# One decoder step on one Trainium2 core: borders of stages cut finer, and low parts of attention's weights on GpSimd

## The chip, the cores and the metric

The kernel runs on one core of a Trainium2 chip. The core has TensorE (matmul), VectorE, ScalarE, GpSimd and SyncE, each with its own queue of instructions that it works off in order; they wait for each other through semaphores. The metric is the device time of one execution in microseconds, the median of three runs.

## The reference

Two decoder layers over a prompt of 1024 tokens and 8 samples of 4 tokens, with the same weights, D = 1024:

```python
# every sub-layer: h = h + post_norm(f(pre_norm(h))), RMS norms over D
# layer 0: gated linear attention (4 heads), then ConvFFN
# shared K/V = rms_norm(h, g_kv) @ w_kv
# layer 1: sliding-window (128) softmax attention with sinks, 16 query heads over 2 K/V heads, then ConvFFN
def conv_ffn(x, prev, w_up, conv_w, conv_b, w_down):
    up = x @ w_up
    u, val = up[..., :D_FF], up[..., D_FF:]              # D_FF = 2816
    c = conv_b + sum of conv_w[j] * u shifted by j        # 3 taps along the sequence
    return (gelu(c) * val) @ w_down, last two rows of u
def sink_attend(q, k, v, bias, valid, sinks):
    s = where(valid, q @ k * HD ** -0.5 + bias, -inf)
    m = maximum(max(s), sink)
    p = exp(s - m)
    return (p / (sum(p) + exp(sink - m))) @ v
```

It returns the two outputs, the GLA states, the last conv rows and the K/V windows.

## The kernel before

Everything is held transposed: channels on the 128 partitions, tokens along the row. The 1056 tokens are two halves, X = 0 with 512 columns and X = 1 with 544 (two chunks of 272); a whole activation of a half is 8 planes. A product in fp32 is made of three matmuls in a rounded type (fp32r): each factor is a high part (`w_hi`, `act_hi`) and a low part (the value less its high part), and the product is low*high + high*low + high*high.

**Weights.** They are cut in 366 blocks of 128x1024, in the order that `weight_order` writes out. Each is loaded by SyncE (`w_load`, two raw slots), rounded by ScalarE (`w_round`, L409), and VectorE subtracts (`w_rest`, L414); `w_hi` and `w_lo` have three slots. `round_after(act, name)` and `rest_after(dve, name)` treat the block three places after the named one. `w_load` of a block waits for the `w_lo` of the block two places before it.

**Order of stages on every engine.** A first norm of half 0; eight GLA turns (4 heads for half 0, 4 for half 1); FFN halves f = 0 and 1 (22 tiles each: an up block `u`, a value block `val`; every two tiles a group of down projections with two `d` blocks, `down_unit` L451, added into `acc` by VectorE, `down_add` L463); attention in 64 steps of one head pair and one block of 128 queries, with query projections, output projections (`ao`) and the samples' part between them; FFN halves f = 2 and 3; and a last norm of half 1. `project` (L431) makes all projections that are no down projections.

**Borders.** Between two stages of a half, `acc` is normed, scaled and added to the residual h, which is read back from DRAM, and then normed again to give the next stage's `act_hi` and `act_lo`. This pass of a half runs while the other half is in a stage, in nine numbered steps that hand-written tables (`ACT_GLA`, `DVE_GLA`, `ACT_STEPS`, `DVE_STEPS`, `PE_STEPS`, `ACT_AT`, `DVE_AT`, `PE_AT`) put at turns, tiles and attention steps: 0 and 1 are squares of half of the planes (`act_square`, folded by `dve_fold`), 2 is the sum over partitions by a matmul with ones (`pe_sum`, L509), the root (`act_rstd`) and the load of half of h, 3 the other half, 4 to 6 the same for the next norm, 7 and 8 the normed planes (`dve_norm` L561), their high part (`act_hi` L570) and the low part on GpSimd (`pool_lo`, L574), which has no other work. `dve_post` scales a pair of planes and adds h to it at once:

```python
dve.wait_ge(po_done, 4 * p - 3 + 2 * m + y)
dve.wait_ge(h_in, 32 * (2 * p - 1 + m))
last = nc.vector.tensor_tensor(a, a, NM[X][:, 2 * y:2 * y + 2], ALU.add)
```

At the start SyncE loads constants, x of half 0, two weight blocks, x of half 1, and then writes the bias rows of attention to DRAM, each 128 times (3 MB), before it goes on with weights. Softmax attention is, for one step on VectorE: scores plus bias (L1719), maximum (L1724), its negative (L1726), reciprocal (L1730), and for half of the steps a copy of the sinks (L1713); ScalarE has the exponentials (L1860) and the scaling (L1869).

Of the kernel before, what the change touches and what calls it, by code (L numbers as in the profile page):

```python
# [15 lines left out]
P = 128  # L16
D = 1024
# [53 lines left out]
KH = KT // 2  # L71


def weight_order():
# [12 lines left out]

    put(("glr", 0), W_GLR)
# [4 lines left out]
    for u in range(2 * H):  # L93
# [4 lines left out]
        if u < 2 * H - 1:  # L98
            for what in "qk":
                put((what, u + 1), gla_row(what, (u + 1) % H))  # L100
            for t in range(2):
                put(("v", u + 1, t), gla_row("v", (u + 1) % H, t))
        for t in range(2):
            put(("o", u, t), gla_row("o", u % H, t))

    def ffn(f):
        w0 = (W_F0, W_F1)[f // 2]

        def tile(g, t):
            b = w0 if g == 0 else w0 + 4 + 6 * (g - 1)  # L110
            bt = b + 2 * t + (2 * t if g else 0)
            put(("u", f, 2 * g + t), bt)
            if f == 1 and 2 * g + t == 11:
                for x in range(2):
                    put(("kv", 0, x), W_KV + x)
            put(("val", f, 2 * g + t), bt + 1)

        def downs(g):
            b = w0 + 4 + 6 * g + 2 if g < FG - 1 else w0 + 4 + 6 * (FG - 1)
            for t in range(2):  # L120
                put(("d", f, g, t), b + t)

        tile(0, 0)
        tile(0, 1)
        for g in range(1, FG):
            tile(g, 0)
            downs(g - 1)
            tile(g, 1)
        downs(FG - 1)

    def att():
        def query(q):
            X, p = divmod(q, 8)
            put(("aq", X, p), W_M1 + HW * (p // 4) + p % 4)

        def downs(k):
            X, d = divmod(k, 4)
            for t in range(2):
                put(("ao", X, d, t), W_M1 + HW * (d // 2) + 4 + 2 * (d % 2) + t)

        query(0)
        for k in range(8):
            query(2 * k + 1)
            if k == 2:
                put(("kv", 1, 0), W_KV)
            if k < 7:
                query(2 * k + 2)
            if k == 2:
                put(("kv", 1, 1), W_KV + 1)
            if k:  # L150
                downs(k - 1)
        downs(7)

    ffn(0)
    ffn(1)
    att()
    ffn(2)
    ffn(3)
# [8 lines left out]
def build(nc, wall, xT, gains, ffnpar, wgate, state, kcT, vc, ck, cv, onehot, masks, smask, bmask,  # L167
# [10 lines left out]
    with ctx:  # L178
# [30 lines left out]
        EPSC = place("eps_col", [P, 1])  # L209
# [2086 lines left out]
```

## Time and profile before

| | |
|---|---|
| median of three runs | 2797.86 us (2793.33 to 2800.45) |
| profiled execution | 2794.6 us, its span 2792.8 us |
| TensorE busy | 2521.1 us, 90% |
| VectorE busy | 1654.8 us, 59% |
| ScalarE busy | 1140.4 us, 41% |
| GpSimd busy | 85.5 us, 3% |
| mean granted TensorE clock | 0.955 |
| DMA | 255 MB, 91 GB/s |

The span goes from the first to the last instruction; a row of a timeline gives start, duration, engine (a q behind it marks its sequencer, where DMAs are issued), line, operation, tiles and count, and in brackets how long the engine had been idle before it and who ended that. "issue" means that the profile shows nothing that ended the wait.

### The profile page before, as it was taken

What the parts mean: (1) busy time and instruction counts of PE and PEld (TensorE: products, weight loads), DVE (VectorE), ACT (ScalarE), POOL (GpSimd) and SP (SyncE); (2) the same over time, 40 slices, a digit from 0 to 9 for tenths busy, and PEclk for the clock granted to TensorE, in tenths of its full rate; (3) what the DMA queues carried; (4) which work ended last, traced back from release to release, by engine and by line L of the source; (5) the groups of instructions that cost most, each with busy time, mean ns of one, the idle gap of its engine ahead of it and who ended that gap; (6) DMA issues with size and microseconds to landing.
All of it is one profiled execution on the core that took longest, in us unless ns stands there. A gap on an engine that the chain in (4) does not pass through costs nothing.

```text
span 2792.8 us, 37637 instructions
## 1 busy us (share of the span) xinstructions
PE 2521.1 (90%) x15437; PEld 2206.9 (79%) x15437; DVE 1654.8 (59%) x2811; ACT 1140.4 (41%) x1792; POOL 85.5 (3%) x22
## 2 busy tenths in 40 slices
PE   2999999998999999999997889878999999999994
PEld 1777888887778879999995666667777888999994
DVE  2677556665665555765555666665665555655554
ACT  2555444343443324333334656553443333333232
POOL 0000000000010000010000110000001000000000
PEclk8999999988999999999998899989999999999997
DMA  7222213322422323323223222221332232332222
GB/s 153 78 67 76 84 63 101 106 85 81 155 78 96 98 76 96 133 74 99 84 84 100 74 90 76 67 93 34 107 129 91 93 98 79 106 118 80 88 91 75
DMA packets 93799, 255.17 MB, mean 91 GB/s; under 512 B 10947, under 2 KB 44204, under 8 KB 91820
## 3 DMA queue, kind: packets, MB, share of 16 engines
q1 hardware_dynamic: 69916, 209.24, 24.1%
q10 hardware_dynamic: 23712, 43.52, 4.4%
q8 instruction: 123, 2.02, 0.3%
q14 instruction: 48, 0.39, 0.0%
HBM read 225.92 MB, written 26.74 MB: 90 GB/s over the span
## 4 chain that ended last, share of the span: by engine, by line
PE 39%; DVE 5%; ACT 4%; issue 3%; DMA 1%; POOL 1%; ACTq 0%; DVEq 0%
PE banks L431 23%; PE banks L451 13%; DMA normed<-h_scratch 1%; ACT w_hi L409 1%; DVE w_lo L414 1%; PE banks L1569 1%; PE banks L1543 1%; ACT probs L1860 1%; PE banks L1555 1%; POOL act_lo L574 1%; DVE normed L561 0%; ACT act_hi L570 0%; DVE hf L1371 0%; DVE stats L1724 0%; ACT normed L488 0%
## 5 line engine op out<-in xcount | busy, mean ns | idle before, releaser
L431 PE MATMUL banks<-act_hi,w_lo 128*128 128x272 f32 (+1 forms) x2952 | 977.1, 331 | 49.5 <-DVE act_lo L574 21.1
L431 PE MATMUL banks<-act_hi,w_hi 128*128 128x272 f32 (+1 forms) x2952 | 963.1, 326 | 0.0
L431 PE MATMUL banks<-act_lo,w_hi 128*128 128x272 f32 (+1 forms) x2952 | 961.8, 326 | 0.0
L409 ACT ACTIVATE w_hi<-w_raw 128x1024 fp32r<-128x1024 f32 x366 | 380.5, 1055 | 778.8 <-PE banks L451 518.4
L414 DVE TENSOR_TENSOR w_lo<-w_raw,w_hi 128x1024 fp32r<-128x1024 f32 x366 | 464.8, 1283 | 375.9 <-ACT w_hi L409 375.7
L431 PEld LDWEIGHTS banks<-act_hi,w_lo 128*128 128x128 f32 x2952 | 562.5, 191 | 112.9 <-issue 27.4
L431 PEld LDWEIGHTS banks<-act_lo,w_hi 128*128 128x128 f32 x2952 | 563.5, 191 | 44.0 <-issue 1.7
L431 PEld LDWEIGHTS banks<-act_hi,w_hi 128*128 128x128 f32 x2952 | 561.7, 190 | 44.0
L463 DVE TENSOR_TENSOR acc<-acc,banks 128x272 f32<-128x272 f32 (+1 forms) x624 | 315.9, 518 | 216.5 <-PE banks L451 212.5
L451 PE MATMUL banks<-h_hi,w_lo 128*128 128x272 f32 (+1 forms) x1056 | 354.9, 336 | 59.0 <-issue 36.1
L451 PE MATMUL banks<-h_lo,w_hi 128*128 128x272 f32 (+1 forms) x1056 | 351.4, 333 | 0.0
L451 PE MATMUL banks<-h_hi,w_hi 128*128 128x272 f32 (+1 forms) x1056 | 351.3, 333 | 0.0
L451 PEld LDWEIGHTS banks<-h_hi,w_lo 128*128 128x128 f32 x1056 | 205.9, 195 | 84.5 <-issue 39.3
L451 PEld LDWEIGHTS banks<-h_lo,w_hi 128*128 128x128 f32 x1056 | 207.4, 196 | 17.0
L451 PEld LDWEIGHTS banks<-h_hi,w_hi 128*128 128x128 f32 x1056 | 205.7, 195 | 16.4
L574 POOL TENSOR_TENSOR act_lo<-normed,act_hi 128x2176 fp32r<-128x2176 f32 (+1 forms) x18 | 85.3, 4739 | 2042.5 <-ACT act_hi L570 2042.5
L1425 ACT ACTIVATE u<-banks 128x512 f32<-128x512 f32 (+2 forms) x132 | 59.0, 451 | 170.7 <-PE banks L431 167.0
L1438 ACT ACTIVATE c<-u,par 128x512 f32<-128x512 f32 (+1 forms) x88 | 73.1, 830 | 95.0 <-issue 89.5
L1860 ACT ACTIVATE probs<-scores,stats 128x257 f32<-128x257 f32 (+1 forms) x128 | 62.4, 489 | 76.9 <-PE banks L1555 39.2
L1348 DVE SCALAR_TENSOR_TENSOR c<-u,par,c 128x512 f32<-128x512 f32 (+1 forms) x88 | 68.0, 773 | 43.1 <-ACT c L1438 43.1
L451 PE MATMUL banks<-o_hi,w_lo 128*128 128x272 f32 (+1 forms) x192 | 68.7, 358 | 23.7 <-DVE acc L463 9.1
L1869 ACT ACTIVATE probs<-probs,stats 128x256 f32<-128x256 f32 (+1 forms) x128 | 56.3, 489 | 68.1 <-DVE stats L1730 67.4
(209 smaller groups left out, 2657.8 us busy)
## 6 DMA issues: line engine op xcount, KB each, us to landing
w_raw<-wall SPq DMA_DIRECT2D x366, 512.0 KB, 3.6
normed<-h_scratch ACTq DMA_DIRECT2D x12, 704.0 KB, 4.7
h_scratch<-acc ACTq DMA_DIRECT2D x3, 2176.0 KB, 8.5
h_scratch<-acc ACTq DMA_DIRECT2D x3, 2048.0 KB, 8.3
gstates<-state ACTq DMA_DIRECT2D x4, 1024.0 KB, 6.2
gla_s<-gstates ACTq DMA_DIRECT2D x4, 1024.0 KB, 4.0
bias<-bias_scratch SPq DMA_DIRECT2D x32, 128.0 KB, 3.6
bias_scratch<-bias_rows SPq DMA_DIRECT2D x1, 3064.0 KB, 36.6
```

Source lines behind the costliest of these rows:

```text
L409: nc.scalar.activation(WH[:, b % RING], WR[:, b % RAW], ACT.Copy).then_inc(w_hi, 1)
L414: nc.vector.tensor_tensor(WL[:, b % RING], WR[:, b % RAW], WH[:, b % RING].bitcast(fp32), ALU.subtract).then_inc(w_lo, 1)
L431: last = nc.tensor.matmul(PS[:, bank, 0:n], w, a[X][:, k, o:o + n], start=(k == 0 and first), stop=(k == KT - 1 and w is wh and a is AH))
L451: last = nc.tensor.matmul(PS[:, bank, 0:w_], w, a[t][:, o:o + w_], start=(t == 0 and x == 0), stop=(t == 1 and x == 2))
L463: nc.vector.tensor_tensor(a, a, PS[:, bank, 0:w_], ALU.add).then_inc(dn_add, 1)
L574: engine.tensor_tensor(AL[X][:, part(m)], NM[X][:], AH[X][:, part(m)].bitcast(fp32), ALU.subtract).then_inc(al_done, 1)
L1348: nc.vector.scalar_tensor_tensor(C[:, 0:cv], U[:, 1:1 + cv], PAR[:, t, 17:18], C[:, 0:cv], ALU.mult, ALU.add).then_inc(cv1, 1)
L1425: last = nc.scalar.activation(U[:, 2 + o:2 + end], PS[:, bank, 0:end - o], ACT.Copy)
L1438: nc.scalar.activation(C[:, 0:cv], U[:, 2:2 + cv], ACT.Identity, bias=PAR[:, t, 19:20], scale=PAR[:, t, 18:19]).then_inc(cb, 1)
L1543: last = nc.tensor.matmul(PS[:, e, x0:2 * WIN], Q1[x, q % 2, i * WIN:(i + 1) * WIN], KG[x, q % 8 // 4, (blk - 1) * WIN + x0:(blk + 1) * WI ...
L1860: last = nc.scalar.activation(EX[:, u, e, x0:], SS[:, u, e, x0:], ACT.Exp, bias=ST[:, r, 2 + e:3 + e], accum_out=ST[:, r, 4 + e:5 + e])
L1869: last = nc.scalar.activation(x, x, ACT.Copy, scale=ST[:, g % 8, 6 + e:7 + e])
```

## The change

- **Start.** The first norm has functions of its own (`act_first_norm`, `dve_first_norm`, `pe_first_norm`): x comes in quarters, each fold goes to a matmul of its own, and the normed planes are made in quarters. The load of half 1's x stands behind the loads of blocks `("v", 0, 0)` and `("r", 0, 0)`; the bias rows have a place of their own in SBUF and are written two at a time from tile 2 of f = 0 on.
- **Joins.** The first `u` and `val` blocks of f = 0 and f = 2 stand before the last down projections of the stage ahead (`pe_first_block`). The last down group of f = 0 and f = 2 stands after the first tile of the next half; that of f = 1 after attention's first query.
- **Passes.** Scaling and residual are separate steps (`dve_scale`, `dve_residual`), h is loaded in quarters, the steps have names, and the tables place them anew; K and V of half 0 move from tile 11 to 13.
- **Attention.** From the second query block on to the last step, GpSimd subtracts the low parts of the weights (`pool_att`, 31 blocks) and its own `pool_lo` of that stage stands in the same queue.
- **End.** The last down group goes chunk by chunk, with squares, sums, root, results and stores by chunk; h of the last pass is loaded ahead into `act_lo`.

```diff
-        def act_h_load(act, i, X, m):
-
-            if m:
-                act.wait_ge(ha_done, 2 * POSTS[i, X] - 1)
+        def act_h_load(act, i, X, y):
+
+            p = POSTS[i, X]
+            if y < 2:
+                act.wait_ge(ps_done, 2 * NORMS[i, "post", X])
             else:
...
+                act.wait_ge(ha_done, 4 * p - 5 + y)
...
+        def dve_residual(dve, i, X, y):
+            p = POSTS[i, X]
+            dve.wait_ge(po_done, 4 * p - 3 + y)
+            dve.wait_ge(h_in[y % 2], 32 * (2 * p - 1 + y // 2))
+            a = ACC[X][:, pair(y)]
+            nc.vector.tensor_tensor(a, a, NM[X][:, pair(y % 2)], ALU.add).then_inc(ha_done, 1)
...
+                else:
+                    pe.wait_ge(os_ev, h + 1)
+                    pe_first_block(pe, 0, "u", FIRST)
...
+                else:
+                    pe_first_block(pe, 0, "u", SECOND)
+                    pe.wait_ge(gq_ms, u + 1)
+                    pe_first_block(pe, 0, "val", ALL)
...
-        PE_STEPS, DVE_STEPS = {3: 2, 7: 6}, {1: 0, 2: 1, 4: 2, 5: 3, 6: 4, 7: 5, 8: 6, 9: 7}
-        ACT_STEPS = {0: 0, 1: 1, 3: 2, 4: 3, 5: 4, 6: 5, 7: 6, 8: 7, 9: 8}
+        PE_FFN = {3: "sum", 9: "Sum"}
+        DVE_FFN = ({1: ("f0",), 2: ("f1",), 4: ("s0", "s1"), 5: ("a1", "s2", "s3"), 6: ("a3",), 7: ("F0",), 8: ("F1",),
+                    10: ("n0a", "n0b"), 11: ("n1a", "n1b")},
+                   {4: ("a0",), 5: ("a2",)})
+        ACT_FFN = ({1: ("sq1",), 3: ("root",), 5: ("h3",), 6: ("Sq0",), 7: ("Sq1",), 9: ("Root",), 10: ("hi0",), 11: ("hi1",)},
+                   {0: ("sq0",), 2: ("h0", "h1"), 4: ("h2",)})
...
+            pool.wait_ge(w_lo, BLK["aq", 0, 1] + RING)
+            for s in range(NIT + 1):
+                k, w = divmod(s, 8)
+                if w == 2:
+                    rest_after(pool, ("aq", (2 * k + 1) // 8, (2 * k + 1) % 8), nc.gpsimd)
+                    if k == 2:
+                        rest_after(pool, ("kv", 1, 0), nc.gpsimd)
+                elif w == 4 and k < 7:
+                    rest_after(pool, ("aq", (2 * k + 2) // 8, (2 * k + 2) % 8), nc.gpsimd)
+                    if k == 2:
+                        rest_after(pool, ("kv", 1, 1), nc.gpsimd)
+                elif w == 0 and k >= 2:
+                    for t in range(2):
+                        rest_after(pool, ("ao", (k - 2) // 4, (k - 2) % 4, t), nc.gpsimd)
+                if s in POOL_LO:
+                    pool_lo(pool, *POOL_LO[s])
...
-            sp.wait_ge(rb_row, 1)
-            sp.dma_start(r_dram.rearrange("(h p m) -> h p m", p=P, m=RL),
-                         RB[:].unsqueeze(1).broadcast_to([NQ, P, RL])).then_inc(rb_out, 16)
...
+        def dve_first_norm(dve):
+            for y in range(4):
+                dve.wait_ge(e_sq, y + 1)
+                x = NM[0][:, pair(y % 2)]
+                if y >= 1:
+                    dve.wait_ge(e_ss, y)
+                nc.vector.tensor_tensor(RS[0][:], x[:, 0], x[:, 1], ALU.add).then_inc(e_f, 1)
...
+            pe.wait_ge(w_lo, BLK["d", 3, FG - 1, 1] + 1)
+            pe.wait_ge(hl, FT * 4)
+            for m in range(2 * KT):
+                if m == KT + KH:
+                    sums(0)
+                down_unit(pe, 1, LAST_DOWNS, m, [BLK["d", 3, FG - 1, t] for t in range(2)],
+                          [HH[:, t] for t in range(2)], [HL[:, t] for t in range(2)], 4 + m % 4, 4)
+            sums(1)
```

## Rows read from the trace of the kernel before

**Rows 1.** The page's section 1: busy time by engine, share of the span, instructions.
```profile
PE 2521.1 (90%) x15437; PEld 2206.9 (79%) x15437; DVE 1654.8 (59%) x2811; ACT 1140.4 (41%) x1792; POOL 85.5 (3%) x22
```

**Rows 2.** Busy time in stretches: start:end, length, busy us (instructions) by engine, granted clock, DMA.
```profile
0.00:62.00 62.00, 13.05 (x28) 7.87 (x29) 19.20 (x23) 15.75 (x12) 0.20 (x4) 0.81 0.79 168
...
653.00:1489.00 836.00, 799.14 (x4816) 718.85 (x4814) 494.62 (x798) 299.16 (x393) 28.18 (x6) 0.98 0.30 96
...
1489.00:1915.00 426.00, 346.87 (x2278) 264.57 (x2278) 268.21 (x542) 248.62 (x596) 28.47 (x6) 0.92 0.25 79
...
1915.00:1946.00 31.00, 24.73 (x195) 21.96 (x196) 14.47 (x35) 9.33 (x22) 0.00 (x0) 0.89 0.11 35
...
2756.00:2793.00 37.00, 2.18 (x4) 1.17 (x4) 15.67 (x18) 7.97 (x6) 0.00 (x0) 0.54 0.37 120
```

**Rows 3.** TensorE's waits over the span: us in total, times, longest.
```profile
PE banks L451 <- issue: 50.3, 15, 8.1
...
PE banks L1569 <- DVE o_lo L1737: 24.6, 6, 6.7
```

**Rows 4.** DMA issues up to us 70, and the timeline of the start.
```profile
bias_scratch<-bias_rows SPq DMA_DIRECT2D x1, 3064.0 KB, 36.6
...
18.41 2.05 PE L509 MATMUL banks<-rstd,ones 128*128 128x512 f32 x2 [12.75 <-DVE rstd L503]
...
23.15 2.74 DVE L561 SCALAR_TENSOR_TENSOR normed<-acc,gain_cols,rstd 128x512 f32<-128x512 f32 x4 [4.89 <-ACT rstd L517]
...
57.06 0.80 PE L431 MATMUL banks<-act_hi,w_lo 128*128 128x512 f32 x1 [21.10 <-DVE act_lo L574]
...
62.24 0.39 PE L431 MATMUL banks<-act_hi,w_lo 128*128 128x512 f32 x1
```

**Rows 5.** TensorE's timeline at the GLA join, and the chain around us 2150.
```profile
639.07 0.57 PE L451 MATMUL banks<-go_hi,w_lo 128*128 128x272 f32 x1 [8.12 <-issue]
...
2142.37 22.30 PE banks L431 x96
```

**Rows 6.** Timelines of TensorE and VectorE in the FFN halves.
```profile
720.45 1.29 DVE L549 TENSOR_TENSOR acc<-acc,normed 128x1088 f32<-128x1088 f32 x1 [1.73 <-DMA normed<-xT]
...
725.70 0.77 PE L451 MATMUL banks<-h_hi,w_lo 128*128 128x512 f32 x1 [4.94 <-issue]
...
780.63 0.70 PE L509 MATMUL banks<-rstd,ones 128*128 128x272 f32 x2 [1.89 <-DVE rstd L503]
...
831.49 4.55 DVE L414 TENSOR_TENSOR w_lo<-w_raw,w_hi 128x1024 fp32r<-128x1024 f32 x1 [2.65 <-ACT w_hi L409]
...
2416.71 0.36 PE L451 MATMUL banks<-h_hi,w_lo 128*128 128x272 f32 x1 [4.29 <-issue]
```

**Rows 7.** Attention from us 1489 to 1946: shares of the chain, then two rows of timelines.
```profile
by line: PE banks L431 18.2%; PE banks L451 16.6%; issue 7.1%; DMA normed<-h_scratch 4.6%; PE banks L1569 4.3%; PE banks L1543 3.6%; ACT probs L1860 3.6%; PE banks L1555 3.3%; DVE stats L1724 2.5%; DVE w_lo L414 2.2%; DVE scores L1719 2.2%;
...
1539.84 0.69 PE L1569 MATMUL banks<-probs_t,v_tok 128*64 128x128 f32 x4 [6.68 <-DVE o_lo L1737]
...
1807.61 1.22 DVE L549 TENSOR_TENSOR acc<-acc,normed 128x1024 f32<-128x1024 f32 x1 [6.74 <-DMA normed<-h_scratch]
```

**Rows 8.** Groups by shape (GpSimd, VectorE), then the timeline beside two GpSimd instructions.
```profile
L574 POOL TENSOR_TENSOR act_lo<-normed,act_hi 128x2048 fp32r<-128x2048 f32 x8 | 36.6, 4578 | 1084.7 <-ACT act_hi L570 1084.7
...
L414 DVE TENSOR_TENSOR w_lo<-w_raw,w_hi 128x1024 fp32r<-128x1024 f32 x366 | 464.8, 1283 | 375.9 <-ACT w_hi L409 375.7
...
1633.43 4.80 POOL L574 TENSOR_TENSOR act_lo<-normed,act_hi 128x2176 fp32r<-128x2176 f32 x1 [33.96 <-ACT act_hi L570]
...
1634.07 4.19 DVE L1713 COPY scores<-sinks_b 128x2 f32<-128x2 f32 x1
...
1651.24 2.82 DVE L1726 TENSOR_SCALAR stats<-stats 128x2 f32<-128x2 f32 x1
```

**Rows 9.** Timeline of the tail.
```profile
2756.17 2.02 ACT L488 ACTIVATE normed<-acc 128x2176 f32<-128x2176 f32 x1 [15.05 <-DVE acc L463]
...
2778.44 10.40 ACTq L1484 DMA_DIRECT2D yT<-acc  x4
```

More of the change, by code:

```diff
@@ L71 @@
 KH = KT // 2
+KV_TILE = 13
 def weight_order():
@@ L102, in weight_order @@
                 put(("v", u + 1, t), gla_row("v", (u + 1) % H, t))
+        if u == 2 * H - 1:
+            ffn_tile(0, 0)
         for t in range(2):
             put(("o", u, t), gla_row("o", u % H, t))
[L106 to L158, printed above, removed]
+    def ffn_layer(l):
+        for f in (2 * l, 2 * l + 1):
+            for t in range(FT):
+                if f % 2 or t:
+                    ffn_tile(f, t)
+                if t % 2 == 0 and t:
+                    ffn_downs(f, t // 2 - 1)
+                elif t == 0 and f % 2:
+                    ffn_downs(f - 1, FG - 1)
+    def query(q):
+        X, p = divmod(q, 8)
+        put(("aq", X, p), W_M1 + HW * (p // 4) + p % 4)
+    def att_downs(k):
+        X, d = divmod(k, 4)
+        for t in range(2):
+            put(("ao", X, d, t), W_M1 + HW * (d // 2) + 4 + 2 * (d % 2) + t)
@@ L159, in weight_order @@
+    ffn_layer(0)
+    query(0)
+    ffn_downs(1, FG - 1)
+    for k in range(8):
+        query(2 * k + 1)
+        if k == 2:
+            put(("kv", 1, 0), W_KV)
+        if k < 7:
+            query(2 * k + 2)
+        if k == 2:
+            put(("kv", 1, 1), W_KV + 1)
+        if k:
+            att_downs(k - 1)
+    ffn_tile(2, 0)
+    att_downs(7)
+    ffn_layer(1)
+    ffn_downs(3, FG - 1)
     return names, rows
@@ L1209, in turn @@
                     nc.scalar.activation(O[:, :, HP:WM], PS[:, 0:2, 0:SAMP], ACT.Copy).then_inc(os_ev, 1)
+                for step in gla_steps(ACT_GLA, u, "outputs"):
+                    act_step(act, *step, 0)
                 if more:
@@ new lines, in dve_ffn, with act_ffn_downs_done @@
+                if f % 2 or t:
+                    rest_after(dve, ("val", f, t))
+                product(f, t)
+                group = ffn_group(f, t)
+                if group is not None:
+                    dve_ffn_adds(dve, *group)
+                    for x in range(2):
+                        rest_after(dve, ("d", *group, x))
+                dve_ffn_lo(dve, f, t)
+        def act_ffn_downs_done(act, f, g):
+            act.wait_ge(dn_full, dn_end((f, g)))
+            for t in range(2):
+                round_after(act, ("d", f, g, t))
```

779 lines of the change are left out of this document (464 added, 315 removed), and 6 rows, old and new, of tables (DVE_AT, DVE_GLA).

## The prediction

> **What bounds the kernel now.** The page's first section comes first: TensorE is busy 2521.1 of 2792.8 us [rows 1]. No matmul is removed (the last sum of squares is cut finer), so what can be won is the 272 us in which TensorE is idle, less what the change costs. The table by stretch shows where these are [rows 2]: 49 of the first 62 us, 37 in the first FFN layer (653 to 1489), 79 in attention (to 1915), 6 where it drains, and 35 of the last 37; the other 66 lie in the GLA turns and the second FFN layer. VectorE is busy 63% and ScalarE 58% of attention: neither is full, so attention waits on chains between engines. The list of what TensorE waited for says what ends the waits [rows 3]: 15 waits of 50.3 us in sum stand in front of down projections, where the profile names no releaser, and 24.6 us in attention are for o_lo. The longest were then followed in the timeline.
>
> **Start.** The 3 MB write of the bias rows takes 36.6 us and is issued at 14.03 us. The weight loads are behind it on SyncE's queue, so the third block is late. ScalarE rounds it ahead of the second half of act_hi, and TensorE stands 21.10 us until 57.06; the first query projection starts at 62.24 [rows 4]. The change writes the rows in eight parts inside the first FFN and lifts the second half's inputs behind two weight loads. I retrace the start with the same rows. x comes in four quarters; folds (0.7 us for two planes of 512) and sums (2.05 us a matmul) alternate, because each fold waits for the sum before it: four rounds of about 2.9 us from us 7.5 on end at 19, against 20.5 now. Root with one table load brings rstd at 21.6. VectorE then has eight norm steps (2.74 us per four), four low parts and one weight low part of 1024 columns (1.28 us each) and a memset: 12.4 us, so query(0) starts near 34. Gain 28, less 1 to 2 for a TensorE that is not warm: 27 (22 to 30).
>
> **Joins of stages.** The last GLA down projection waits 8.12 us for normed outputs [rows 5]. Now the first FFN up and value blocks stand ahead of it, 48 matmuls; 96 take 22.30 us [rows 5], so 11.1 us of work. Half of `u` stands before the sum of squares and delays the chain by 2.8 us, and the low part of the second half of act_hi ends some 0.7 us after it is wanted. The downs then start at 642.8, not 639.1: 11.1 - 3.7 = 7.4, plus 1 because the matmuls behind the wait start slow (0.57 us for 272 columns): 8.5 (6 to 10). Inside each FFN layer the last down group (4.43 and 4.44 us) now has the next half's first tile in front: 8 (6 to 9). Into attention (4.65) a query projection of 5.6 us covers it: 4.5 (3 to 6). Out of attention the window of 31 us holds 6.3 idle [rows 2] and 11.1 us of work to put there: 6 (3 to 7). The last of these waits (3.14) stays.
>
> **Tile 4 of each FFN half.** The four waits there are 4.94, 4.11, 4.97 and 4.29 us, first and last in [rows 6]. VectorE meets the residual's load (1.73 us of wait at 720.45), and four more steps and the weight's low part stand behind it before TensorE resumes at 725.70. The change starts the load at tile 2, puts the root ahead in tile 3, and lets only the scaling stand before the weight's low part: 16 of 18.3 (12 to 18). The second sum of squares moves from tile 7 to 9: 4.5 of the 5 us of rows like the one at 780.63 (3 to 5). At tile 10 and in the second half's norm steps a weight low part is held by GpSimd (4.55 us at 831.49, with 3.17 us of TensorE wait behind it, twice; smaller ones in the second half, 9 in sum) [rows 6]. The new order puts the weight ahead of act_hi, but conv now meets GpSimd: 6 (-2 to 10).
>
> **Attention, loads.** The chain of the 457 us from 1489 on has 4.6% on the residual's load, 21 us; VectorE waits 6.74 us for it at 1807.61, and TensorE 6.68 us at 1539.84, the last of three waits of 16.3 us there [rows 7]. Loads now start two and six steps ahead of the root and stand in quarters: 19 (10 to 22).
>
> **Attention, GpSimd.** 31 weight low parts leave VectorE. All 366 have a mean of 1283 ns, so 40 us; on the chain they hold 2.2%, 10 us [rows 7]. GpSimd takes 4578 ns for 2048 columns [rows 8], so 2.3 us for 1024, 71 us in all. No row shows GpSimd on weights, but its five long instructions of attention show the price beside VectorE. While one runs (1633.43 to 1638.23), a two-element copy that has a median of 148 ns takes 4.19 us and ends with it; the sign change of the maxima takes 2.82 us at 1651.24 instead of 0.17 [rows 8]. Additions from PSUM that start beside it keep their length. So a short VectorE instruction, which every softmax step has on its chain, stands for the rest of a GpSimd instruction. I laid 2.3 us behind each of the 31 roundings in the trace, the first at 1504.98 and the last at 1919.30: 14 meet such an instruction, and the delays sum to 21.4 us. As half of VectorE's work there is on the chain, 11 lost against 10 won: 0 (-21 if all count and nothing is won, to +10). A weight block itself is not late: three slots lie ahead of TensorE, and a projection takes 5.6 us.
> The Trainium skill, "SBUF — State Buffer", section "Who interferes with whom", calls the ports of the two engines one exclusive lock, held for a whole instruction, and lets a VectorE instruction with one SBUF input and no two-port mode pass; the trace agrees (4.19 us in the place of 0.15). It speaks against this part of the change: that is the first rival below.
>
> **Tail.** From the last matmul of the downs, 37 us pass [rows 2]: two squares of 2.02 and folds (9.6 us in all until the sum), a load that waits for the buffer, four scale-and-add pairs with a second load, then a 1.1 MB store [rows 9]. Now the downs run chunk by chunk. The first chunk's squares, sum and root lie under the second's (1.8 us of sum matmuls stand between them), the residual is loaded 14 us early, and behind the last matmul are one add, one square, eight results, one fold and a store of a quarter. A result is two steps of 272 columns and an add of 544, from neighbours 0.48 and 0.72 us: 1.8 with latency. 1.2 + 8 x 1.8 + 0.5 + 2.5 = 18.6, plus 1.8: 20.4. Gain 16 (13 to 19).
>
> **Small costs.** ScalarE issues 25 more DMAs (0.48 us each, 12 us over all stages, mostly where it idles over 40%). Eight parts of the bias write take 4.6 us each, a weight load 3.6, and a load has two blocks of 5.6 us: covered. If not, each costs up to 1. I take -2 (0 to -8).
>
> **Sum.** 27 + 8.5 + 8 + 4.5 + 6 + 16 + 4.5 + 6 + 19 + 0 + 16 - 2 = 113.5. The profiled execution took 2794.6 (1.8 around its span), so 2681; the median is 3.3 above it: 2684. All low ends give 47, all high ends 146: 2652 to 2751.
>
> **Rivals.**
> *The lock decides attention.* Every instruction that meets GpSimd waits on the chain, and the work taken off VectorE wins nothing: 21.4 us, 2705. Where two low parts follow each other behind the output blocks, 4.6 us at once, up to 10 more. For it: the two waits in [rows 8]. Against: in 17 of 31 places nothing meets it. 2705 to 2715, chance 0.17.
> *Waits are only displaced.* Finer steps make more waits between in-order engines; half of tile 4, the sums and the loads (45 us) comes back: 23. For: the profile shows which wait ended last, not the next one. 2707, chance 0.13.
> *VectorE was the pace of attention.* 24.6 us of TensorE's waits there are for o_lo [rows 3], and the shared queue delays the additions too; with 40 us less work ahead of them another 27, two thirds of it, go. 2657, chance 0.13.
> *Slower than before.* GpSimd's low part is wanted by the third next block and frees the raw slot; if VectorE's two-input instructions keep it from starting and each weight is late by more than 113.5 / 31 = 3.7 us, the gain is gone; at 5 us it is 2839. Against: its 18 instructions now last 4.5 to 4.9 us with VectorE beside them. Chance 0.03.
>
> **Numbers.** The forecast has 0.54: 2684, by itself 2668 to 2700. The range reaches to the lock and to the quick attention: 2652 to 2732. A measurement tells about 0.3%, 8 us, from no change. Every case but the last is over 60 us faster: faster 0.96, same 0.01, slower 0.03.
>
> **What would show it.** Query projections from us 34; no TensorE wait over 2 us at tile 4 and at the joins; no wait for h_scratch in attention; about 20 us behind the last down matmul. GpSimd would show 31 instructions of 2.3 us, and VectorE's two-element instructions a tail up to 2.3 us; attention (query to the last output block) near 415 us. If these stand and attention is above 430, the lock decided; if the FFN layers keep over 50 us of idle TensorE together, the waits moved.

## The result, and the profile after

The changed kernel takes 2753.86 us (median of 4 runs, 2746.97 to 2759.79) against 2798.76 (2793.33 to 2800.45) for the kernel before, now of four runs: ratio 0.9842, 95% interval 0.9815 to 0.9869. It is 45 us faster, where 114 were forecast; the range (2652 to 2732) missed it by 22 us. The profiled execution took 2752.62 with a span of 2750.7.

Section 1 of the page after, beside [rows 1]:

```profile
PE 2532.1 (92%) x15455; PEld 2214.3 (81%) x15455; DVE 1660.6 (60%) x2796; ACT 1147.1 (42%) x1810; POOL 160.7 (6%) x53
```

TensorE is idle 219 us, 53 less than before, but it is busy 11 us longer, with hardly any work added. The table by stretch, cut at the last addition of each stage: start, the four feed-forward networks (the FFN halves f = 0 to 3) with attention between the second and third, tail. The GLA turns, 40.1 to 626.6, are left out here.

```profile
0.00:40.10 40.10, 23.09 (x59) 12.11 (x60) 18.88 (x25) 18.65 (x21) 0.20 (x4) 1.00 0.49 161
626.60:1023.80 397.20, 380.65 (x1645) 308.02 (x1644) 234.06 (x304) 146.92 (x178) 10.10 (x2) 0.98 0.35 109
1023.80:1447.90 424.10, 410.72 (x3147) 404.12 (x3145) 266.28 (x493) 151.23 (x215) 18.34 (x4) 0.99 0.29 94
1447.90:1949.50 501.60, 392.19 (x2498) 305.12 (x2499) 281.81 (x544) 259.82 (x619) 103.11 (x37) 0.87 0.23 70
1949.50:2328.40 378.90, 374.34 (x1646) 304.31 (x1645) 233.98 (x304) 147.30 (x178) 10.11 (x2) 1.00 0.34 106
2328.40:2733.90 405.50, 395.36 (x3079) 392.11 (x3079) 236.87 (x473) 136.81 (x208) 0.00 (x0) 0.99 0.30 96
2733.90:2750.70 16.80, 1.88 (x6) 0.59 (x4) 13.19 (x26) 4.83 (x8) 0.00 (x0) 0.67 0.41 133
```

The same cuts of the kernel before, and what each stage won once the work that moved over a border is allowed for. The moved work is priced with [rows 5]: 96 matmuls in 22.30 us, so 11.15 for a first tile of 48 and 5.57 for a query projection of 24. A first tile of a second half (96 short matmuls) is 12.06. "Combined" is the best of the first experiments; it comes below.

| stage | before | after | won | forecast | combined | won |
|---|---|---|---|---|---|---|
| to the first query copy | 68.0 | 40.1 | 27.9 | 27 | 40.3 | 27.7 |
| GLA | 585.3 | 586.5 | 10.0 | 8.5 | 585.5 | 11.0 |
| network 1 | 394.0 | 397.3 | -2.4 | | 380.1 | 14.8 |
| network 2 | 441.8 | 424.0 | 11.3 | | 423.9 | 11.4 |
| attention | 457.1 | 501.6 | -38.9 | 25 | 463.5 | -0.8 |
| network 3 | 393.0 | 378.9 | 15.0 | | 379.8 | 14.1 |
| network 4 | 416.9 | 405.5 | -0.7 | | 405.3 | -0.5 |
| four networks together | | | 23.2 | 39 | | 39.8 |
| tail | 36.7 | 16.8 | 19.9 | 16 | 16.8 | 19.9 |

(39 are the terms 8, 16, 4.5, 6 and the 4.5 of the join into attention, whose wait stood ahead of network 2's last additions. 25 are the loads' 19 and the 6 out of attention.) The columns sum to 42 and, with the small costs of -2, to 113.5. So start, GLA and tail came near their terms, and networks 2 to 4 together won 25.6. Two places lost: **network 1**, and **attention**.

*Network 1.* SyncE, ScalarE and TensorE in the timeline behind the first bias part:

```profile
626.97 0.76 SPq L1273 DMA_DIRECT2D bias_scratch<-bias_rows  x1
628.48 32.23 SPq L410 DMA_DIRECT2D w_raw<-wall  x6
660.75 0.65 SPq L1273 DMA_DIRECT2D bias_scratch<-bias_rows  x1
...
645.99 1.06 ACT L415 ACTIVATE w_hi<-w_raw 128x1024 fp32r<-128x1024 f32 x1 [4.69 <-DMA w_raw<-wall]
...
681.15 1.06 ACT L415 ACTIVATE w_hi<-w_raw 128x1024 fp32r<-128x1024 f32 x1 [5.67 <-DMA w_raw<-wall]
...
648.35 0.79 PE L437 MATMUL banks<-act_hi,w_lo 128*128 128x512 f32 x1 [5.53 <-DVE w_lo L420]
...
695.94 0.77 PE L460 MATMUL banks<-h_hi,w_lo 128*128 128x512 f32 x1 [3.45 <-issue]
```

The weight issued at 628.48, right behind the part, is there at 645.99: 17.5 us for a load that takes some 4. TensorE stands 5.5 us until 648.35, and 3.5 until 695.94.

*Attention.* What TensorE waited for there (us in total, times, longest):

```profile
PE banks L460 <- DVE acc L472: 21.2, 8, 5.7
PE banks L437 <- ACT rstd L520: 14.2, 2, 7.1
PE banks L1719 <- DVE s_scores L1867: 12.9, 2, 6.8
PE banks L437 <- issue: 10.3, 2, 9.6
PE banks L1617 <- issue: 8.8, 1, 8.8
...
PE banks L1643 <- DVE o_lo L1821: 4.9, 3, 1.8
```

The wait for o_lo, 24.6 us in [rows 3], is down to 4.9, as forecast. The first five rows have taken its place. The 8.8 us stand ahead of the first scores, and the 9.6 us ahead of the keys and values of step 16. GpSimd's group for the weights, beside [rows 8]:

```profile
L420 POOL TENSOR_TENSOR w_lo<-w_raw,w_hi 128x1024 fp32r<-128x1024 f32 x31 | 74.8, 2426 | 417.3 <-ACT w_hi L415 417.3
```

31 instructions of 2.4 us, as forecast (2.3). Two of them stand beside VectorE's chain of the sample softmax:

```profile
1766.77 4.64 POOL L420 TENSOR_TENSOR w_lo<-w_raw,w_hi 128x1024 fp32r<-128x1024 f32 x2 [26.04 <-ACT w_hi L415]
...
1767.28 1.86 DVE L1856 TENSOR_TENSOR s_stats<-s_stats,s_sinks 128x1 f32<-128x1 f32 x1
1769.17 2.26 DVE L1858 TENSOR_TENSOR s_stats<-s_sinks,s_stats 128x1 f32<-128x1 f32 x1
...
1775.04 0.57 PE L437 MATMUL banks<-act_hi,w_lo 128*128 128x272 f32 x1 [7.15 <-ACT rstd L520]
```

One-column instructions, 0.16 us each in the kernel with VectorE's low parts (e1, below), end with GpSimd's two instructions. Behind them ScalarE makes the exponentials and then the root, and TensorE waits 7.15 us for the root, where the same wait in the kernel before was 3.3.

### The profile page after: what moved, and what is told of

It reads as the page before. It is cut to its first block and busy times, and to the rows that moved or that the text cites. A ratio compares the mean times of both kernels' runs of the same rounds, so it can differ in the third digit from the quotient of the medians.

```text
span 2750.7 us, 37795 instructions
## 1 busy us (share of the span) xinstructions
PE 2532.1 (92%) x15455; PEld 2214.3 (81%) x15455; DVE 1660.6 (60%) x2796; ACT 1147.1 (42%) x1810; POOL 160.7 (6%) x53
## 5 line engine op out<-in xcount | busy, mean ns | idle before, releaser
L437 PE MATMUL banks<-act_hi,w_lo 128*128 128x272 f32 (+1 forms) x2952 | 985.8, 334 | 51.1 <-ACT rstd L520 14.2
L420 DVE TENSOR_TENSOR w_lo<-w_raw,w_hi 128x1024 fp32r<-128x1024 f32 x335 | 432.2, 1302 | 391.3 <-ACT w_hi L415 391.0
L437 PEld LDWEIGHTS banks<-act_hi,w_lo 128*128 128x128 f32 x2952 | 568.5, 193 | 116.7 <-issue 59.0
L437 PEld LDWEIGHTS banks<-act_lo,w_hi 128*128 128x128 f32 x2952 | 569.4, 193 | 44.2 <-issue 1.7
L437 PEld LDWEIGHTS banks<-act_hi,w_hi 128*128 128x128 f32 x2952 | 567.6, 192 | 44.6
L460 PEld LDWEIGHTS banks<-h_lo,w_hi 128*128 128x128 f32 x1056 | 204.9, 194 | 16.3
L420 POOL TENSOR_TENSOR w_lo<-w_raw,w_hi 128x1024 fp32r<-128x1024 f32 x31 | 74.8, 2426 | 417.3 <-ACT w_hi L415 417.3
```

The costliest lines, as they stand in the source:

```text
L420: engine.tensor_tensor(WL[:, b % RING], WR[:, b % RAW], WH[:, b % RING].bitcast(fp32), ALU.subtract).then_inc(w_lo, 1)
L437: last = nc.tensor.matmul(PS[:, bank, 0:n], w, a[X][:, k, o:o + n], start=(k == 0 and first), stop=(k == KT - 1 and w is wh and a is AH))
L460: last = nc.tensor.matmul(PS[:, bank, 0:w_], w, a[t][:, o:o + w_], start=(t == 0 and x == 0), stop=(t == 1 and x == 2))
```

## The experiments

All ran beside the kernel before. Ratios are to it.

| run | median us (range) | ratio, 95% interval |
|---|---|---|
| after | 2753.9 (2747.0 to 2759.8) | 0.9842, 0.9815 to 0.9869 |
| e1_dve_low | 2720.6 (2717.8 to 2724.1) | 0.9722, 0.9709 to 0.9735 |
| e2_bias_16rows | 2733.0 (2731.4 to 2738.9) | 0.9770, 0.9756 to 0.9785 |
| e3_before_gpsimd | 2833.4 (2830.3 to 2835.6) | 1.0123, 1.0110 to 1.0137 |
| e4_sp_join | 2745.8 (2742.8 to 2750.6) | 0.9813, 0.9798 to 0.9827 |
| e5_combined | 2696.3 (2694.2 to 2699.9) | 0.9629, 0.9604 to 0.9655 |
| e6_pool_order | 2741.4 (2740.7 to 2745.2) | 0.9792, 0.9766 to 0.9817 |
| e7_lock_alone | 2735.2 (2734.6 to 2740.2) | 0.9771, 0.9745 to 0.9797 |
| e8_bias_start | 2752.7 (2749.7 to 2757.4) | 0.9827, 0.9801 to 0.9852 |
| e9_no_gpsimd | 2690.2 (2687.0 to 2696.1) | 0.9621, 0.9602 to 0.9640 |
| e10_late_loads | 2694.7 (2688.8 to 2697.7) | 0.9630, 0.9611 to 0.9649 |
| e11_loads_step5 | 2700.7 (2699.0 to 2704.6) | 0.9648, 0.9632 to 0.9664 |
| e12_bias_4rows | 2752.9 (2748.6 to 2754.4) | 0.9830, 0.9814 to 0.9847 |
| e13_loads_halves | 2704.6 (2698.2 to 2709.8) | 0.9656, 0.9632 to 0.9680 |
| e14_bias_8rows | 2734.0 (2728.5 to 2735.0) | 0.9758, 0.9738 to 0.9778 |
| e15_gpsimd_ordered | 2714.6 (2711.2 to 2717.3) | 0.9689, 0.9670 to 0.9709 |

### GpSimd in attention

**Low parts back on VectorE** (e1), in the changed kernel:

```
 # pool_att
-                if w == 2:
-                    rest_after(pool, ("aq", ...), nc.gpsimd)
...
 # dve_att, behind biased(s)
+                if w == 2 and k < 8:
+                    rest_after(dve, ("aq", (2 * k + 1) // 8, (2 * k + 1) % 8))
...
```

> The changed kernel with the low parts of the attention's weights subtracted on VectorE again, at the places in its order where the kernel before has them; everything else stays, GpSimd's activation low parts too. Theory (GpSimd's lock on VectorE's small operations and its own order of work cost the attention): the attention, 501.6 us from the end of the second feed-forward network in the changed kernel, falls by 30 to 45 us, the kernel from 2754 to 2710 to 2724; VectorE's work runs long by 30 us instead of 67. Rival (the rewritten tables and the added work of the first tile cost it, not GpSimd): the attention stays within 8 us, kernel 2746 to 2762. Rival of the forecast (GpSimd helps, VectorE is the pace): the kernel gets slower, over 2762.

Measured 2720.6: 33 us less, in attention (501.6 to 470.6 us). The theory holds; the rival that GpSimd helps has the wrong sign. Over the whole kernel VectorE's instructions still run long by 52 us, not 30 (each instruction's length over the median of its shape, where it is over by a quarter and 0.1 us, summed; 67.5 in the changed kernel, 30.2 before). 16 of the 52 lie in attention, where the kernel before had 8: the new order puts more short ones beside GpSimd's six remaining low parts. The other 36 lie outside attention, where the kernel before had 23.

**The kernel before with that alone** (e3): `rest_after` on GpSimd, all borders as before.

> The kernel before with one thing of the change: the low parts of the attention's weights on GpSimd, in the place of its order that the change gives them; all borders stay as before. Theory (lock and in-order queue cost): slower than before by 20 to 40 us, 2818 to 2840, all of it between the end of the second network and the end of the attention. Forecast's own term (no cost, from 21 us of gain to 10 us of loss): 2778 to 2808. If the loss is under 10 us here and over 30 in the run with VectorE's low parts, then GpSimd's cost comes only together with the new order of steps.

Measured 2833.4, 35 us slower, all of it in attention (457.1 to 492.5 us). GpSimd's cost is the same in both orders of steps, 33 and 35 us; the forecast had it at 0.

**The lock by itself** (e7), on top of e1:

```
+            def idle_low(b):
+                pool.wait_ge(w_hi, b + RING + 1)
+                for _ in range(2):
...
+                    nc.gpsimd.tensor_tensor(DM[:], DM[:], DM[:], ALU.subtract)
```

> The changed kernel with the low parts of the attention's weights on VectorE, and GpSimd made to do, at the same places of its order and released by the same high parts, two subtractions of 128x512 each on a spare tile that nobody reads or waits for, where it had one low part of 128x1024. Nothing depends on them, so what they cost over the run with VectorE's low parts alone (2721) is their presence beside VectorE, not their lateness. Theory (most of GpSimd's cost is that VectorE's instructions are held while it works): 8 to 20 us over 2721, 2729 to 2741, and VectorE's instructions run over by 15 to 40 us more than in that run. Rival (its cost is that the low parts come later, in order and 2.4 us long): within 5 us of 2721.

Measured 2735.2: 14.5 us over e1, with VectorE's instructions long by 74.5 us in place of 51.9. GpSimd was busy somewhat longer with the idle work than with the real one (87.0 us in 62 instructions against 74.8), so by this run the lock's share of the 33 is 12 to 15 us. But the idle instructions are 1.1 to 1.4 us long and let VectorE in sooner than the real ones of 2.4. The two statistics of the sample softmax that took 1.86 and 2.26 us in the changed kernel, here:

```profile
1760.34 4.46 POOL L1939 TENSOR_TENSOR idle<-idle 128x512 f32<-128x512 f32 x4 [24.59 <-ACT w_hi L418]
...
1760.84 0.55 DVE L1859 TENSOR_TENSOR s_stats<-s_stats,s_sinks 128x1 f32<-128x1 f32 x1
1761.43 0.16 DVE L1861 TENSOR_TENSOR s_stats<-s_sinks,s_stats 128x1 f32<-128x1 f32 x1
```

TensorE's two waits for the root sum to 6.1 us in place of 14.2. So 12 to 15 is what the lighter work costs, and the real one may cost more; e15 below bears on it.

**One entry of GpSimd's order** (e6):

```
-        POOL_LO = {13: (2, "kv", 1, 0), 15: (2, "kv", 1, 1), ...
+        POOL_LO = {13: (2, "kv", 1, 0), 16: (2, "kv", 1, 1), ...
```

> The changed kernel with one entry of GpSimd's own order moved: the low part of the second half of the attention's key and value activations comes behind the two weight low parts of step 16, not ahead of them. Theory (GpSimd works in its written order, and a weight low part that is ready waits behind an activation low part that isn't): the stall of 9.6 us ahead of the keys and values at step 16 falls to 3 to 6, the kernel from 2754 to 2747 to 2751. Rival (that stall is the lock's, or is paid again two steps later): the stretch from step 16 to step 24 stays at 76 us, and the kernel at 2752 to 2757.

GpSimd's timeline in the changed kernel, and then in e6, with TensorE's wait behind it:

```profile
1547.80 4.77 POOL L581 TENSOR_TENSOR act_lo<-normed,act_hi 128x2176 fp32r<-128x2176 f32 x1 [6.12 <-ACT act_hi L577]
1552.53 4.66 POOL L420 TENSOR_TENSOR w_lo<-w_raw,w_hi 128x1024 fp32r<-128x1024 f32 x2
...
1554.97 0.56 PE L437 MATMUL banks<-act_hi,w_lo 128*128 128x272 f32 x1 [9.62 <-issue]
```

```profile
1542.80 5.67 POOL L420 TENSOR_TENSOR w_lo<-w_raw,w_hi 128x1024 fp32r<-128x1024 f32 x2 [2.67 <-ACT w_hi L415]
1548.42 4.85 POOL L581 TENSOR_TENSOR act_lo<-normed,act_hi 128x2176 fp32r<-128x2176 f32 x1
...
1545.74 0.36 PE L437 MATMUL banks<-act_hi,w_lo 128*128 128x272 f32 x1 [1.94 <-issue]
```

The high parts were rounded by 1545.2. In the changed kernel GpSimd is idle, waiting for act_hi, until 1547.80, and takes the weights only after that low part. One number moved in a table takes the wait from 9.6 to 1.9 us and 12.4 us off the kernel, more than expected. In the profile attention falls from 501.6 to 490.9 us:

```profile
1449.20:1940.10 490.90, 389.31 (x2498) 303.01 (x2499) 289.80 (x545) 259.65 (x619) 104.24 (x37) 0.89 0.23 72
```

Idle time is 7.8 us less, and 7.7 of it is this wait; the same 2498 matmuls take 2.9 us less, at a mean granted clock of 0.89 in place of 0.87.

### The bias parts

**Sixteen rows a part** (e2):

```
-            sp.dma_start(r_dram.rearrange(...)[first:end],
-                         RB[first:end].unsqueeze(1).broadcast_to([end - first, P, RL])).then_inc(rb_out, 16)
+            sp.dma_start(r_dram.rearrange(...)[:, 8 * first:8 * end],
+                         RB[:].unsqueeze(1).broadcast_to([NQ, 8 * (end - first), RL])).then_inc(rb_out, 16)
```

> The changed kernel with the eight parts of the bias cut the other way: each part reads all 16 head rows and writes 16 of the 128 copies, where it read 2 rows and wrote all 128 copies; bytes and places are the same. Theory (a part that reads two partitions only is slow at its source, some 18 us a piece, and the weight loads of the first network wait behind it): a part takes 5 to 9 us, the first network falls from 397 to 383 to 388 us, kernel 2739 to 2745. Rival (the write into DRAM or the sum of bytes is what holds the weights up): parts still take over 14 us and the kernel stays at 2751 to 2757. Rival (the first network loses by its GpSimd low parts and the halo copy at tile 10): the parts get shorter and the first network stays within 4 us.

Measured 2733.0, 21 us less; a part lands in 5.7 us by the page; network 1 falls from 397.3 to 379.9. The theory holds, and the gain is larger than expected: 17.4 of the 21 us are in network 1, where TensorE's waits of 0.9 us and more fall from 15.6 to 5.6 us in sum. That is what is left without any part there (5.4 in e8, below).

**Four rows and eight rows** (e12, e14; `RB[h:h + 4]` to 64 copies, `RB[h:h + 8]` to 32):

> The changed kernel with each of the eight parts of the bias reading 4 of the 16 rows and writing 64 of the 128 copies; bytes and places are the same. Theory (a part takes as long as the rows that it reads from let it: two rows some 17 us, sixteen rows 6): a part holds the weight loads up half as much, the first network falls to 384 to 392 us, kernel 2738 to 2748. Rival (any part with fewer than 16 rows costs the same, or only 2 rows are slow): the first network at 397, or at 380, us.

> The changed kernel with each of the eight parts of the bias reading 8 of the 16 rows and writing 32 of the 128 copies; bytes and places are the same. With 2 and with 4 rows the first network took 397 us, with 16 rows 380. Theory (rows that lie next to each other share one way out at some 25 GB/s, whatever number of transfer engines reads them): 397 again, 2750 to 2756. Rival (it depends on how many rows or engines a part has, with a step between 4 and 16): 380 to 390 us, 2733 to 2745.

Four rows: 2752.9, network 1 at 397.4, as with two. Eight rows: 2734.0, network 1 at 380.0, as with sixteen. My theory for four (time in proportion to rows) fell, and so did the one for eight (neighbours always share). Windows in which nearly nothing but a part is on its way, in the changed kernel (2 rows), with 4 rows and with 8; the last two numbers are the DMA engines' mean share and GB/s:

```profile
640.00:644.00 4.00, 2.82 (x13) 1.95 (x11) 2.62 (x3) 1.30 (x3) 0.00 (x0) 1.00 0.12 26
```

```profile
640.00:644.00 4.00, 4.00 (x19) 3.14 (x17) 2.26 (x3) 2.72 (x3) 0.00 (x0) 1.00 0.21 25
```

```profile
634.00:636.00 2.00, 2.00 (x10) 1.64 (x9) 1.24 (x2) 0.55 (x2) 0.00 (x0) 1.00 0.44 50
```

26 and 25 GB/s for two and four rows, 50 for eight: the rate doubles from four rows to eight and not from two to four. A part is 256 packets of 1532 bytes in the trace; from the first to the last of them pass 13 to 15 us with two rows, 14 with four, 6 to 7 with eight and 3 to 4.5 with sixteen. The Trainium skill, "SBUF — State Buffer", section "Door 1: The DMA port swizzle", has four neighbouring partitions on one of 16 ports of about 27 GB/s each; the trace agrees, with 25 and 26 GB/s for one such group and 50 for two. The Trainium skill, "DMA: Bandwidth & Descriptors", section "Why a DMA increments its semaphore by 16 and not by 1", takes the largest number of transfer engines, at most 16, that divides the outermost dimension of both sides; the shares of 0.12, 0.21 and 0.44 for two, four and eight rows are near 2, 4 and 8 of 16.

**One piece at the start** (e8): the eight parts gone, one write of all rows behind the first loads.

> The changed kernel with the bias written in one piece behind the first loads, where the kernel before has it, in place of eight parts in the first network. Theory (it holds up the first weights at the start, and the eight parts hold them up in the first network): the first query copy of the first layer moves from 40.1 to 46 to 58 us, the first network falls from 397 to 381 us, so the kernel comes to 2740 to 2755. Rival (the start's gain of 28 us comes from the finer steps of the first norm alone): first query copy at 40 to 43 us and the kernel near 2738.

Measured 2752.7, the changed kernel's time. The first query copy comes at 58.8 us, and network 1 is at 379.7. So what moving the write won (18.7 us) its eight narrow parts lost again (17.6). Of the start's 27.9 us 18.7 are the write's; the other 9.2 are those of the finer steps and of the second half's inputs, which e8 leaves behind the two weight loads. Which of the two has how much is not shown.

### SyncE's wait

**One block later** (e4):

```
-                elif name == ("aq", 0, 2):
+                elif name == ("aq", 0, 3):
                     sp.wait_ge(cn, FT * 2)
```

> The changed kernel with one thing moved on SyncE: its wait for the last weight low part users of the second network and the seven loads behind it (bias rows, masks) stand after the load of the next attention query block, not ahead of it. Theory (the first scores wait 8.9 us for the high parts of the last down projection's successor block, whose load is queued behind this wait): the stall ahead of the first score falls from 8.9 us to 2 to 4, kernel shorter by 4 to 7 us, 2747 to 2750. Rival (the masks and bias of the first steps then come later and the first steps wait for them instead): no difference, 2752 to 2756, with a new wait on a DMA in the first three steps.

SyncE's, ScalarE's and TensorE's timeline in the changed kernel, then TensorE's in e4:

```profile
1447.43 1.75 SPq L2086 DMA_DIRECT2D bias<-bias_scratch  x4
...
1450.65 6.63 SPq L410 DMA_DIRECT2D w_raw<-wall  x3
...
1454.61 1.06 ACT L415 ACTIVATE w_hi<-w_raw 128x1024 fp32r<-128x1024 f32 x1 [6.12 <-DMA w_raw<-wall]
1455.57 0.58 ACT L1954 ACTIVATE q<-banks 128x512 f32<-128x512 f32 x1
...
1456.25 0.80 PE L1617 MATMUL banks<-kg,q 64*128 64x128 f32 x4 [8.85 <-issue]
```

```profile
1454.50 0.80 PE L1617 MATMUL banks<-kg,q 64*128 64x128 f32 x4 [2.62 <-issue]
```

In the changed kernel the first query's block stands ahead of the last down blocks in the order of weights. Their rounding makes ScalarE round one block further on, and SyncE issues that one only after its wait for the last down group and seven loads. The query's copy is behind that rounding. Measured 2745.8, 8 us less, of which this wait is 6.2.

### All three, and what is left

**Combined** (e5: e1, e2 and e4).

> The changed kernel with three edits together: the attention's weight low parts back on VectorE, the parts of the bias read from 16 rows each, and SyncE's wait and seven loads one block later. Theory (three separate causes in three stages): their gains of 33.2, 20.9 and 8.1 us add up, 2692, from 2685 to 2699; the attention near 466 us, the first network near 381 us. Rival (the gains overlap, since a stall taken away only moves the wait): above 2702.

2696.3: the gains add, to within 4 us. This is 102 us below the kernel before.

**The change's GpSimd, repaired** (e15: e2, e4, e6).

> The changed kernel as it is, GpSimd with the attention's weight low parts, with three repairs: GpSimd's own order (the key and value low part behind the two weight low parts of step 16), the bias parts of 16 rows and SyncE's wait one block later. Theory (gains add, and GpSimd then costs what the lock takes and the later low parts of the last steps): 2753.9 less 12.4, 20.9 and 8.1 is 2712, from 2706 to 2718, 16 us over the same kernel with VectorE's low parts (2696). Rival (once the queue is in order GpSimd is no worse than VectorE): 2693 to 2700.

2714.6: with its queue in order GpSimd still costs 18 us over VectorE. TensorE's waits in attention, where e5 has 6.5 us for the root and 8.0 for the samples' scores:

```profile
PE banks L437 <- ACT rstd L520: 14.3, 2, 7.2
PE banks L1719 <- DVE s_scores L1867: 12.9, 2, 6.8
```

That is 12.7 us more. The first stands again behind statistics of 1.86 and 2.26 us, and ahead of the second a fold of VectorE's takes 3.40 us beside GpSimd's two instructions and 1.22 without them. The only wait for a low part of GpSimd's is 4.2 us, where VectorE's low part was waited for 3.1. So these traces lay most of the 18 us to held instructions, and some 1 us to low parts that come later.

**No GpSimd in attention** (e9: e5 with `lo_rest(nc.vector, dve, ...)` for the six activation low parts too).

> The combined kernel (attention's weight low parts on VectorE, bias parts of 16 rows, SyncE's wait one block later; 2696) with the six low parts of the activations in the attention on VectorE as well, one step later each; GpSimd does nothing in the attention. Theory (what is left of the attention's excess is partly VectorE's instructions held by GpSimd's six low parts of 4.8 us: the copy of the sinks of 3.9 us at step 60, a statistics instruction of 2.8 us): VectorE takes 15 us of work more and loses some 20 us of delays, the stall of 5.7 us at step 60 falls to 2 or less; 2688 to 2695. Rival (VectorE's added work takes the place of the delays): 2696 to 2704.

2690.2, the lowest median; its interval overlaps e5's, so the runs do not tell the two apart. In the profile attention is 457.1 us against 463.5, as long as in the kernel before, and the wait at step 60 went from 5.7 to 2.0 us.

**Loads behind the root** (e10), **at the old steps** (e11), **in halves at the old steps** (e13), each on e5:

```
-        ACT_AT = {0: ("sq0",), 1: ("sq1",), 2: ("h0", "h1"), 3: ("root",), 5: ("h2",), 6: ("h3",), ...
+        ACT_AT = {0: ("sq0",), 1: ("sq1",), 3: ("root", "h0", "h1"), 5: ("h2",), 6: ("h3",), ...           # e10
+        ACT_AT = {0: ("sq0",), 1: ("sq1",), 3: ("root",), 5: ("h0", "h1"), 6: ("h2", "h3"), ...            # e11
+        ACT_AT = {0: ("sq0",), 1: ("sq1",), 3: ("root",), 5: ("h0", "h1"), 7: ("h2", "h3"), ...            # e13
```

The second pass (steps 38 to 60) is changed alike. e10 issues the first loads two steps ahead of where the kernel before has them. e13 also has VectorE wait for both quarters of a half, and in the first pass puts two of its additions one step later.

> The combined kernel (2696) with the loads of the first two quarters of the stored activations behind the root of the norm in both passes of the attention, as the kernel before has them, in place of ahead of it. Theory (the forecast's term for the loads: they were late for VectorE, and earlier issue removes its waits): VectorE waits for them again and the value products wait behind it, 8 to 19 us over 2696, 2704 to 2715. Rival (the early loads bought nothing, the stalls moved elsewhere anyway): within 4 us of 2696.

> The combined kernel (2696) with the loads of the stored activations issued at the very steps of the kernel before: the first two quarters at steps 5 and 49, the last two at steps 6 and at 50 and 51. (The run with the loads behind the root left them two steps earlier than that, and VectorE never waited.) Theory (the forecast's term for the loads is right in kind): VectorE waits for them again, as the kernel before did for 4.0, 2.3, 6.7 and 1.4 us in the attention, and 5 to 14 us of it reach the end, 2701 to 2710. Rival (TensorE's idle time moves to other waits whether they are there or not): within 4 us of 2696.

> The combined kernel (2696) with the stored activations loaded by halves and as late as in the kernel before: two quarters at a time, at steps 5 and 7 and at 49 and 51, the sums on VectorE waiting for both quarters of a half. Theory (the forecast's term is right in kind and too large, since in the second pass other waits follow that cover it): 5 to 10 us over 2696, 2701 to 2706, nearly all of it in the first pass (steps 0 to 24), and VectorE waits for the loads about 14 us, as before. Rival (the whole term of 19 us is there, and something else in the attention eats it): 12 to 20 us, 2708 to 2716.

VectorE's waits for the load in e11, in e13, and in attention before, where the second row is its wait for GpSimd:

```profile
DVE acc L556 <- DMA normed<-h_scratch: 5.1, 2, 4.3
```

```profile
DVE acc L558 <- DMA normed<-h_scratch: 9.2, 3, 4.3
```

```profile
DVE acc L549 <- DMA normed<-h_scratch: 14.4, 4, 6.7
DVE normed L561 <- POOL act_lo L574: 9.7, 2, 5.6
```

e10 costs nothing: issued two steps before they are wanted the loads are there. e11 costs 4 us. e13 brings 9 us of VectorE's 14 back and costs 8 us by the medians but 1.2 by the profiled spans, and its interval overlaps e5's. In the profiles attention alone is 463.5 us in e5 and e10, 466.9 in e11 and 467.2 in e13, so 3.4 and 3.7 us more. The term is between 1 and 8 us; 19 lies above all three, though none brings all 14 us of VectorE's waits back.

## Why the prediction was wrong

**Start (27), GLA join (8.5), tail (16): right.** 27.9, 10.0 and 19.9 by the table. At the GLA join the wait of 8.12 us is gone; but the GLA stage, which no experiment but e8 touches, is between 581.9 (e9) and 591.7 us (e4) long in the other profiles, so the 10.0 is known to some 5 us. Of the tail's 20.4 us the forecast had 18.6 behind the last down matmul; they were 17.3, because a result takes 1.6 us, not 1.8.

**Networks (39): right in the sum, but for the small costs.** Combined they won 39.8. Only 30 of these are idle time (65.0 us before, 34.6 in the combined kernel, in the four together); the other 9.5 are matmuls that took less time, in networks 1 and 3 at a mean granted clock of 1.00 where it was 0.98. The forecast had added up waits alone, so that its sum fits is in part luck. In the combined kernel the four waits at tile 4, those of the second sum and the two inside the layers are gone, and so is the one of 3.2 us at tile 10 of networks 1 and 3. But the first tiles of these two now wait 4.9 and 4.5 us for a weight's low part, and network 2 keeps two waits for additions, 4.6 and 3.5 us, where it had five smaller ones of 8.9 in sum. The step that failed stands under "small costs": "eight parts of the bias write take 4.6 us each ... covered". That was an eighth of the 36.6 us of [rows 4], and so took the rate of 16 rows for a part of two. A part runs at 25 GB/s, so 13 to 15 us, and the weight behind it comes 14 us late: 21 us lost by the medians, 17.4 in network 1 (e2), where at most 8 were allowed.

**Join into attention: a new wait was not seen.** The forecast had a query projection cover 4.65 us; it did, but did not follow ScalarE's extra rounding to SyncE's queue, where the loads of bias and masks stand ahead of that block. 8 us (e4).

**Attention, GpSimd (0): wrong, and the largest term: -33.** Two errors. The first is the balance of 11 us lost against 10 won. With GpSimd's queue in order and the real low parts the loss is 18 us (e15), near the 21.4 us that the 14 meetings summed to; that only half of it is on the chain was assumed. The 10 us won by taking the work off VectorE show in no run: even with the queue in order attention is 17 us longer than with the weights' low parts on VectorE. Whether the gain was nothing or was eaten, no run separates. The second: "a weight block itself is not late: three slots lie ahead" left out what stands ahead of it in GpSimd's own order. e6 gave 12.4 us back with one entry moved. 18 and 12.4 leave 3 of the 33 us, less than the runs tell apart.

**Attention, loads (19): wrong, 1 to 8.** The views that it rested on were read one step too far. The chain's 21 us are more than all of VectorE's waits for the load, 14.4 us. Of the three waits of 16.3 us up to 1539.84 the first, 4.2, was for ScalarE's probabilities, and it is still there (4.9 us in the combined kernel). Two of the six waits for o_lo (3.5 and 5.9 us) had behind them VectorE's 9.7 us for GpSimd's low part, not the load. And in the second pass VectorE's longest wait, 6.74 us [rows 7], was worth only 2.5 us to TensorE, behind which waits for additions and roots of 3 to 4 us followed whether the load was early or not. The attention of the combined kernel, and the waits in it that replace the one for o_lo:

```profile
1429.80:1893.30 463.50, 384.76 (x2498) 297.77 (x2499) 290.99 (x576) 259.89 (x619) 28.43 (x6) 0.91 0.24 75
```

```profile
PE banks L460 <- DVE acc L472: 20.7, 8, 5.7
PE banks L1719 <- DVE s_scores L1867: 8.0, 2, 4.2
...
PE banks L1643 <- DVE o_lo L1821: 4.5, 3, 1.8
```

The same stretch before:

```profile
1489.10:1946.20 457.10, 371.80 (x2474) 286.71 (x2475) 282.81 (x574) 258.05 (x618) 28.47 (x6) 0.92 0.24 76
```

20 us of waits for o_lo went, and idle time fell from 85.3 to 78.7 us only: waits for additions rose from 14.2 to 23.2 us, those for s_scores from 6.1 to 8.0. The 5.7 us at step 60 are the clearest: before, VectorE waited there for GpSimd to let go of a buffer; now the copy of the sinks is held 3.9 us by the same low part. Against these 6.6 us stands a busy time 7.4 us longer than the 5.6 us of added matmuls, at a mean clock of 0.91 between the two levels, 0.92 before. Why it fell is not settled.

**Out of attention (6): wrong, about 1.** From VectorE's last scores to the end of attention TensorE is idle 7.2 us before and 6.4 in the combined kernel. The first tile's blocks stand behind the wait for s_scores (3.8 us in both) in TensorE's order, so they lengthen the stretch and do not fill it.

**The rivals.** The lock rival named the place and, by e15, nearly the price of the lock alone (21.4 us, 18 measured); what it left out is GpSimd's queue. Waits were displaced too, mostly in attention, where 20 us of them bought 6.6 of idle time. The bias parts and SyncE's wait came on top, and no rival held them. The slower case's rule (a weight late by 3.7 us each) did not come: the one pair that was late, by over 7 us, was the queue's doing.

## What to carry to other kernels

An engine that looks free is free only at certain points: before moving work to it, lay the work into its own written order and ask what each entry ahead waits for, then count the other engine's short instructions beside it. The price of a piece of a transfer is that of its own shape, not its share of the whole: here pieces from 2 or 4 of 16 source partitions cost some 20 us, pieces from 8 or 16 nothing that showed. A wait that the profile names last is worth only what is left once the wait behind it shows; in a chain between four engines 20 us of such waits went and idle time fell by 7.

## What the runs showed of the hardware that I had not expected

- A DMA from 2 or 4 neighbouring partitions ran at 25 to 26 GB/s, and a 512 KB load issued behind one from 2 was ready after 17.5 us; from 8 partitions it ran at 50, and from 16 it landed 383 KB in 5.7 us.
- GpSimd subtractions that nobody reads cost the kernel 14.5 us for 87 us of GpSimd work. Instructions of 2.4 us held VectorE's one-column statistics for 1.86 and 2.26 us; beside ones of 1.1 us the same two took 0.55 and 0.16.
- With more waits in a stretch the same matmuls took longer: 392.2 us in attention at a mean granted clock of 0.87 with 109 us idle, 384.8 at 0.91 with 79, for 2498 instructions each.
